# Weight block sums: two of four made by accumulating DMAs from GpSimd instead of by VectorE

## The reference

```python
def half_ffn(x, i, k):
    h = rms_norm(x, norm_g[i, 2 * k])
    return x + 0.5 * swiglu(h, ffn_w_gate[i, k], ffn_w_up[i, k], ffn_w_down[i, k])

def swiglu(h, w_gate, w_up, w_down):
    return (jax.nn.silu(h @ w_gate) * (h @ w_up)) @ w_down
```

## Time and profile before

| | |
|---|---|
| runs | 2117.47 us median (2117.15 to 2117.64) |
| profiled execution, first to last instruction | 2115.8 us |
| TensorE busy | 2098.3 us (99%), 17064 matmuls |
| VectorE busy | 1523.0 us (72%) |
| ScalarE busy | 996.4 us (47%) |
| GpSimd busy | 145.2 us (7%) |
| mean granted clock of TensorE | 0.999 of full speed |
| DMA | 203.65 MB, 206228 packets |

### The profile page before, as it was taken

The page is one execution under the profiler, slowest core; times in us unless marked ns, Lnnn a source line. Parts: engine busy times, 40 slices in busy tenths (PEclk is TensorE's granted clock), DMA queues, the critical chain, the costliest instruction groups (busy, mean ns, idle before and its releaser), DMA issues.

```text
span 2115.8 us, 42925 instructions
## 1 busy us (share of the span) xinstructions
PE 2098.3 (99%) x17064; PEld 2036.3 (96%) x17064; DVE 1523.0 (72%) x2282; ACT 996.4 (47%) x1565; POOL 145.2 (7%) x155
## 2 busy tenths in 40 slices
PE   8999999999999999999999999999999999999999
PEld 8999999999999999999999999998768799999999
DVE  7887695336367879587978869579665568796783
ACT  6445353442135636255644535445563456354451
POOL 0000001222020000000000000111121210000000
PEclk9999999999999999999999999999999999999999
DMA  5233233322323333233332323341322133333232
GB/s 177 90 100 119 77 103 100 100 80 81 96 66 98 103 109 99 99 100 114 97 119 95 124 69 110 120 119 31 90 70 99 42 81 91 100 100 120 80 113 68
DMA packets 206228, 203.65 MB, mean 96 GB/s; under 512 B 12359, under 2 KB 201076, under 8 KB 205844
## 3 DMA queue, kind: packets, MB, share of 16 engines
q1 hardware_dynamic: 202938, 196.67, 28.9%
q0 software_dynamic: 2848, 4.86, 1.3%
q10 hardware_dynamic: 314, 0.37, 0.1%
HBM read 194.42 MB, written 2.66 MB: 93 GB/s over the span
## 4 chain that ended last, share of the span: by engine, by line
PE 97%; DVE 1%; ACT 1%; issue 0%; DMA 0%; SPq 0%; DVEq 0%
PE main L700 43%; PE side L749 23%; PE main L749 17%; PE side L1283 2%; PE main L1045 2%; PE main L1213 1%; PE side L1253 1%; PE side L1135 1%; PE main L1115 1%; PE side L959 1%; PE main L1292 1%; PE side L1085 1%; PE side L983 1%; PE main L1198 1%; PE main L1200 0%; PE main L1199 0%
## 5 line engine op out<-in xcount | busy, mean ns | idle before, releaser
L749 PE MATMUL side<-xw_hi,w_hi 128*128 128x260 f32 x1344 | 380.8, 283 | 0.9 <-DVE x L1936 0.8
L700 PE MATMUL main<-h_hi,w_lo 128*128 128x260 f32 x1888 | 380.1, 283 | 0.0
L700 PE MATMUL main<-h_hi,w_hi 128*128 128x260 f32 x1888 | 380.0, 282 | 0.0
L749 PE MATMUL side<-xw_hi,w_lo 128*128 128x260 f32 x1344 | 379.7, 283 | 0.0
L700 PE MATMUL main<-h_lo,w_hi 128*128 128x260 f32 x1888 | 379.3, 282 | 0.0
L749 PE MATMUL side<-xw_lo,w_hi 128*128 128x260 f32 x1344 | 378.2, 281 | 0.0
L700 PEld LDWEIGHTS main<-h_hi,w_hi 128*128 128x128 f32 x1888 | 290.8, 188 | 0.1
L700 PEld LDWEIGHTS main<-h_hi,w_lo 128*128 128x128 f32 x1888 | 290.7, 188 | 0.0
L700 PEld LDWEIGHTS main<-h_lo,w_hi 128*128 128x128 f32 x1888 | 290.1, 188 | 0.0
L749 PE MATMUL main<-xw_hi,w_hi 128*128 128x260 f32 x1008 | 286.8, 285 | 0.0
L749 PE MATMUL main<-xw_lo,w_hi 128*128 128x260 f32 x1008 | 285.8, 284 | 0.0
(11 more groups left out here) (450 smaller groups left out, 3619.7 us busy)
## 6 DMA issues: line engine op xcount, KB each, us to landing
raw<-in_ffn_w_up SPq DMA_DIRECT2D x44, 1024.0 KB, 5.2
raw<-in_ffn_w_gate SPq DMA_DIRECT2D x43, 1024.0 KB, 5.1
raw<-in_ffn_w_down SPq DMA_DIRECT2D x32, 1024.0 KB, 5.2
raw<-in_gmlp_w_in SPq DMA_DIRECT2D x16, 1024.0 KB, 5.4
raw<-in_ffn_w_down SPq DMA_DIRECT2D x16, 768.0 KB, 4.4
raw<-in_gmlp_w_out SPq DMA_DIRECT2D x8, 1024.0 KB, 5.2
raw<-in_mla_w_o SPq DMA_DIRECT2D x8, 1024.0 KB, 5.3
over<-in_cache_mla SPq DMA_DIRECT2D x64, 104.0 KB, 1.9
```

Source lines behind the costliest of these rows:

```text
L700: mm = nc.tensor.matmul(into[:, half, 0:HALF], w[:, k, m * P:(m + 1) * P], moving[:, k, half * HALF:(half + 1) * HALF], start=(k == 0 and ...
L749: mm = nc.tensor.matmul(into[j], w_tiles(w, j)[:, k, :], moving[:, k, j, :], start=(j in (0, 1) and k == 0 and i == 0), stop=(k == 3 and i ...
```

## The change

Two of the four sums are made by DMA. Each fast chunk is loaded by five DMAs instead of one, in runs of 512 B instead of 1 KB, so that each block is contiguous in SBUF; block r1 is loaded twice, once into `raw` and once into `sums_w`. When all five have landed, GpSimd issues two accumulating DMAs of 256 KB from SBUF to SBUF: r3 onto the copy of r1 in `sums_w` ("inner"), and r0 onto r1 in `raw` ("outer"). `sums_outer` is gone. VectorE's `sums_second` now waits for the inner DMA. The rest of tiles 4 and 5, one instruction of 1024 columns before, is two of 512, as is its high part on ScalarE. The order of tiles 1 and 2 is swapped in slot 1, where the pair lies the other way round.

```diff
 # SyncE
+def load_fast(slot, w, c0, free):
+    sp.wait_ge(lo_done, free)
...
+    sp.dma_start(block(raw_block(slot, 3)), part(3)).then_inc(raw_in[slot], 16)
+    sp.dma_start(block(sums_w[:, 2 * slot, :]), part(1)).then_inc(outer_in[slot], 16)
+    for r in range(3):
+        sp.dma_start(block(raw_block(slot, r)), part(r)).then_inc(outer_in[slot], 16)
 # GpSimd, called once for each fast chunk, in the order of the chunks
+def add_weights(s, raw_ready, w):
+    pool.wait_ge(raw_in[s], raw_ready)
+    pool.wait_ge(outer_in[s], 16 * (w - 2 * s) + 64)
+    pool.dma_start(sums_w[:, 2 * s, :], raw_block(s, 3), accum_op=ALU.add).then_inc(inner_added[s], 16)
+    pool.dma_start(raw_block(s, 1), raw_block(s, 0), accum_op=ALU.add).then_inc(outer_added[s], 16)
 # ScalarE
+def fast_third(s, t, w):
+    act.wait_ge(tile_done, t)
+    act.wait_ge(outer_added[s], 4 * (w - 2 * s) + 16)
+    nc.scalar.activation(w_block(w_hi, 4), raw_block(s, 1), ACT.Copy)
     act.wait_ge(weights_summed, w + 2)
+    nc.scalar.activation(w_block(w_hi, 5), sums_w[:, 3, :], ACT.Copy).then_inc(hi_done, 1)
 # VectorE
-def sums_outer(s, raw_ready, rested=None):
-    dve.wait_ge(raw_in[s], raw_ready)
...
-    nc.vector.tensor_tensor(sums_w[:, 0:4:2, :]..., parts[:, 0:4:3],
-                            parts[:, 1:2].to_broadcast([P, 2, 4, P]), ALU.add).then_inc(weights_summed, 1)
+def sums_second(s, w, rested=None):
+    dve.wait_ge(inner_added[s], 4 * (w - 2 * s) + 16)
...
+    nc.vector.tensor_tensor(sums_w[:, 1, :], sums_w[:, 2 * s, :], raw_block(s, 0), ALU.add).then_inc(weights_summed, 1)
+def rest_third(s, l):
+    dve.wait_ge(hi_done, l)
+    take_rest(w_block(w_lo, 4), raw_block(s, 1), w_block(w_hi, 4))
+    take_rest(w_block(w_lo, 5), sums_w[:, 3, :], w_block(w_hi, 5), lo_done)
 def fast_chunk(s, ...):   # VectorE, the next chunk is fast too
-    sums_outer(1 - s, raw_ready, l + 4)
     rest_raw(s, 6, 3, l + 5)
-    sums_second(1 - s, w + 3)
+    sums_second(1 - s, w + 2, l + 4)
     rest_raw(1 - s, 0, 0, l + 6)
-    sums_last(1 - s, w + 3)
+    sums_last(1 - s, w + 2)
```

More of the change, by code:

```diff
@@ L105, in ffn_past @@
                    evac=8 * fast + 4 * plain + 8 * groups, h=2 * pairs, act=2 * pairs, norm=1, rms=1, sums=0 if last else KD,
-                   snap=6 * fast, wsum=6 * fast, rows=2 * fast + 8 * groups, xg=16 + KD if plain else 17,
+                   snap=6 * fast, wsum=4 * fast, rows=2 * fast + 8 * groups, xg=16 + KD if plain else 17,
                    xh=20 + KD if plain else 21, blocks=16, added=0 if plain else 16 * (KD - 2),
@@ L481, in w_tiles, with raw_block, weights_at, added_pair @@
             return w_block(w, j).rearrange("p (i c) -> p i c", c=P)
-        def raw_parts(s):
-            return raw[:, s, :].rearrange("p (i r c) -> p r i c", r=4, c=P)
+        def raw_block(s, r):
+            return raw[:, s, r * BL:(r + 1) * BL]
+        def weights_at(s, j):
+            return 3 - j if s == 1 and j in (1, 2) else j
+        def added_pair(s):
+            return sums_w[:, s:s + 2, :].rearrange("p a c -> p (a c)")
         wkv_flat = wkv[:, :, :].rearrange("p h n -> p (h n)")
@@ L1811, in _ @@
                 if h == 11:
-                    act.wait_ge(ssq_set, 1)
+                    act.wait_ge(key_parts_set, 1)
                     act.wait_ge(scale_set, 1)
@@ L1880, in _ @@
                 if h == 0:
-                    act.wait_ge(pv_summed, 1)
+                    act.wait_ge(os_done, 1)
                     act.wait_ge(sd_inv, 2)
@@ L1952, in sums_second, with sums_last @@
-            def sums_second(s, w):
+                nc.vector.tensor_tensor(sums_w[:, 1, :], sums_w[:, 2 * s, :], raw_block(s, 0), ALU.add).then_inc(weights_summed, 1)
+            def sums_last(s, w):
                 dve.wait_ge(weights_summed, w + 1)
-                nc.vector.tensor_tensor(sums_w[:, 3, :].rearrange("p (i c) -> p i c", c=P),
-                                        sums_w[:, 2, :].rearrange("p (i c) -> p i c", c=P), raw_parts(s)[:, 0],
-                                        ALU.add).then_inc(weights_summed, 1)
@@ L1959, in sums_last @@
[L1959 to L1963, removed]
-                                        ALU.add).then_inc(weights_summed, 1)
+                nc.vector.tensor_tensor(sums_w[:, 3, :], sums_w[:, 1, :], raw_block(s, 2), ALU.add).then_inc(weights_summed, 1)
             def rest_raw(s, j, r, l):
@@ L2031, in first_up @@
                 low, high = slice(0, HALF), slice(HALF, TOK)
-                sums_second(0, w + 3)
+                sums_second(0, w + 2, l + 4)
                 rest_raw(0, 0, 0, l + 6)
@@ L2049, in first_up, with fast_chunk @@
                                                ALU.mult).then_inc(evac_done, 1)
[L2050 to L2055 removed]
+                rest_third(0, l + 9)
+            def fast_chunk(s, t, e, l, w, sn, into, by, after, ready=None, held=None, kept=None, rest_late=False):
                 rest_raw(s, 6, 3, l + 5)
                 if after == "fast":
[L2058 removed]
+                    sums_second(1 - s, w + 2, l + 4)
                     rest_raw(1 - s, 0, 0, l + 6)
[L2060 removed]
+                    sums_last(1 - s, w + 2)
                 else:
@@ L2157, in down @@
                 for i in range(4):
-                    if i == 2 and fast:
-                        sums_outer(n % 2, 16 * (n // 2 + 3))
                     if i == 3 and fast:
@@ L2734, in add_norm_squares, with ffn @@
                     pool.dma_start(square_sum[:], square[:, k % 2, :], accum_op=ALU.add).then_inc(sum_added, 16)
-            def ffn(after, final=False):
+            def ffn(at, after, final=False):
+                n, w = at.chunk, at.wsum
+                for g, pairs in enumerate(FF_GROUPS):
+                    rest = pairs - 2 if n == 0 else pairs
+                    for i in range(pairs - rest, pairs):
+                        if g or i:
+                            add_weights(0, 16 * (n // 2 + i + 1), w)
+                        add_weights(1, 16 * (n // 2 + i + 1), w + 2)
+                        w += 4
+                    n += 2 * pairs + 4
                 if final:
```

228 lines of the change are left out of this document (111 added, 117 removed).

## The result

The changed kernel takes 2172.3 us (median of 4 runs, 2166.07 to 2175.26), against 2117.3 for the kernel before beside it (2115.89 to 2117.64): a ratio of 1.0257, 95% interval 1.0239 to 1.0274. It is 55 us slower. The forecast was no change, 2116.7 with a range up to 2150; what came is close to its rival (a), at the size that it gave for a chain of 13 us (2173).

A forecast was written before the change was run, and what follows sets the result against it. TensorE alone was taken to set the time in fast chunks, with VectorE's relief off the path: 2115.8 - 0.8 = 2115.0 profiled, plus 1.7 for the runs, 2116.7 us. Range 2116 to 2119 for no effect, up to 2150 with a late chain.

The forecast's parts named there:

- rival (a): Load-to-inner-sum chain over 11.14 us, so tile 6 waits for the second eviction in up chunks; 2173 at 13 us; chance 0.25.
- What goes: VectorE loses `sums_outer`, 102.6 us, gains 12.9 from split rests, falling to 1433 us; gain at most 0.8 us.
- The deadline: Second eviction, due before tile 6's weight load, has 0.24 us slack; `sums_second` must start by 4.81 us into the chunk.
- the limit of 11.14: Longest chain, in us, from first load issue to inner sum that still lets `sums_second` start by 4.81 us.
- How long five loads take: First issue to landing of a chunk's five loads: 1.9 us latency plus 4.3 transfer, 6.2 us, bounds 5.8 and 10.1.
- the add's 4.2: Inner accumulating DMA on GpSimd: 3.86 us with issue and wake-up, plus 0.3 for the outer's overlap; bounds 3.3 and 5.5.
- the margin of 0.7 us: Room between the forecast chain of 10.4 us and the 11.14 us allowed; called the weakest number.
- Rival (b): DMA engines become the bound: at 51 ns a packet a chunk needs 11.2 us of 10.10; +95 us, 2213; chance 0.03.
- Rival (c): VectorE keeps GpSimd from issuing its DMAs: 2.4 us more, chain 12.8 us, +50 us, 2167; chance 0.04.
- the port rule: GpSimd can't start a DMA while VectorE holds both shared SBUF ports; inner add some 2.5 us more; not used in the sum.
- (d): Faster: relieved VectorE lets TensorE close its gaps, only 0.8 us in fast chunks, so no gain over 0.2%; chance 0.04.
- (e): VectorE's waits grow, so relief becomes idle time; the forecast's own picture, given no separate chance.

The follow-up runs named there:

- the run with two hops: The kernel whose inner add waits for only two loads, with two DMAs of 4 bytes, each waited for, ahead of every inner add: 2302.0 us, ratio 1.0873.

## Why the prediction was wrong, point by point

- **What goes**: right. VectorE 1432.1 against 1433; the relief is worth nothing, as the kernel with the early inner add shows (84 us less on VectorE than before, ratio 0.9996).
- **The deadline**: right. The first thing late is the second eviction at tile 6, `sums_second` to its end took 3.70 us as worked out, and at a median of 11.06 us the waits there were 2.6 us in all, which fits the limit of 11.14.
- **How long five loads take**: the step that failed. I gave 6.2 us up to landing and counted GpSimd's wake-up in the add's 4.2. Undisturbed, the last of the five lands at 7.07: the fifth issue is where I had it, at 2.1, but I took its landing at 3.7 from a load among four, and it takes 4.9. With the wake-up, the load up to GpSimd's issue takes 7.59 (the kernel with the inner add alone) and the add 3.41, which is 11.0 instead of 10.4: the packet's price was nearly right (28.4 ns, not 26.8), and the margin of 0.7 us shrank to 0.1. In the kernel itself it took 8.89 and 3.83. The missing 1.3 us and 0.4 us go with the outer add, and are the collision with the adds: the load of the next chunk is issued 9.8 to 10.5 us after the last one, when the adds (issued at 7.6 or later, the outer landing 5.6 us after issue) are in flight. I had added up the engines' share for the chunk (70%) and priced the load as if alone; an average of 70% says nothing about who meets whom. Both kinds of DMA suffer: loads of 256 KB take 4.6 (gate) and 5.5 us (up) where undisturbed they take 4.3, the outer add 5.6 instead of 3.3. The Trainium skill, "DMA: Bandwidth & Descriptors", section "Queues, rings and completion order", says that each DMA engine takes turns between the queues it has work for, packet by packet. The traces fit that, though no row shows the turns: a 512 B packet of a load takes 28.6 ns in the mean over the run with the loads alone and no outer sum, and 29.7 in the changed kernel, so the packets are hardly slower while the loads land later.
- **It feeds itself.** A late chain puts its adds into the next load, which makes the next chain late; the prediction had nothing of this kind. It is read from rows (1171.89 to 1180.17 above), and no experiment holds a chain late with its adds kept off the next load. It is the reading under which a hop of 2.5 us, ahead of a chain with room to spare, can cost 65 us (2182.8 against 2117.4).
- **Rival (a)** had the mechanism and the instruction, but its number is in good part luck. It gave "about 30" waits, all in up chunks, and took the other slot as covered by their stalls; 30 x (12.97 - 11.14) = 55 us for 55 measured. The 33 waits are 15 in up chunks (16.2 us) and 18 in gate chunks (23.2 us, with the longest), 1.2 us each in the mean and not 1.83. Some 8.5 us are the lower clock, which was not in that sum.
- **Rival (b)** fell: a 512 B packet costs 28.4 ns and not the 51 of a 1 KB one, and traffic as such costs nothing. **Rival (c)** fell too: GpSimd's issues of the inner add take 0.88 us in the mean beside a busy VectorE, as in the earlier trace rows (the outer's take 1.22, begun before the inner's is over, and 0.89 where they stand alone), so nothing of the port rule weighed there shows in this order. **(d)** and **(e)** went as said.
- The chance of 0.25 for (a), with a margin of 0.7 us on a chain of four links of which no row showed one, was too low.

## What to carry to other kernels

When a sum is moved from an engine to a DMA, the price is a longer chain, not busy time: draw it from first issue to last consumer, and lay the transfers of neighbouring chunks over it, for a DMA is priced by what flies beside it. Let each link wait only for what it uses: the inner add waited for five loads where two were needed, and with that wait gone the whole loss was gone. A relieved engine is worth something only where it sets the time.

## What was not expected of the hardware

- A wait of TensorE of 5.67 us is followed by 3.8 us at granted clock 0.50, 223 ns a matmul; over the run with two hops, 66 us of busy time came on top of the waits.
- The five issues of SyncE are themselves slower beside adds in flight. The last three, one row in the timeline, have a median of 1.56 us in the kernel with the loads alone. In the changed one it is 1.6 where no add is in flight at the first issue and 2.8 where one is more than 1 us from landing, as in these two:

```profile
1174.48 2.70 SPq L562 DMA_DIRECT2D raw<-in_ffn_w_up  x3
1185.08 3.12 SPq L562 DMA_DIRECT2D raw<-in_ffn_w_gate  x3
```

- A DMA of 4 bytes inside SBUF, waited for, cost GpSimd 2.5 and 3.85 us in two chunks in a row, with loads in flight both times; the median of 84 is 2.9.
